# HGRN head 0: forget and query units multiplied together, cleared buffers moved, next head's units spread by halves

## The reference, cut to what matters

```python
h = h + 0.5 * swiglu(rmsnorm_2(h, ffn1_norm), ffn1_w_in, ffn1_w_out)
u = rmsnorm_2(h, mix_norm)
hq, hf, hi, hg = columns of (u @ w_in)       # 8 heads of 128 columns each
log_f = logaddexp(log(lb), log1p(-lb) + log_sigmoid(hf))
k_h = -expm1(log_f)                           # 1 - f
q_h = silu(hq) * 128 ** -0.5
# S_t = diag(f_t) S_{t-1} + k_t^T v_t ; o_t = S_t^T q_t, in chunks of 64
o_h = rmsnorm_2(o, hgrn_out_norm) * silu(hg)
```

## Time and profile before

| | us |
|---|---|
| median of 3 runs | 3306.32 (3302.76 to 3309.76) |
| the profiled execution | 3309.65 |
| its span in the trace | 3307.7 |
| start of the first matmul of head 0's F | 1693.85 |
| start of head 0's level 0 on PE | 1719.94 |
| start of head 1's level 0 on PE | 1751.44 |
| granted TensorE clock over the span | 0.984 |

### The profile page before, as it was taken

One profiled execution on the slowest core, in us unless ns is written; L12 is line 12 of the kernel. 1 busy time (PEld: TensorE's weight loads), 2 busy tenths in 40 slices (PEclk: granted clock), 3 DMA queues, 4 the chain that ended last, 5 costly groups with the idle time before them and its releaser, 6 DMA issues.

```text
span 3307.7 us, 44803 instructions
## 1 busy us (share of the span) xinstructions
PE 3184.6 (96%) x16754; PEld 2628.3 (79%) x16754; DVE 1573.9 (48%) x2197; ACT 1408.4 (43%) x2471; POOL 1587.1 (48%) x1361
## 2 busy tenths in 40 slices
PE   7889999999999999999989998999999999999998
PEld 5657888877688888788878887888888888888887
DVE  5883433136634321434148887655555543234421
ACT  3354343325843333343236565545555432243332
POOL 5345444655554457444553324444444445464454
PEclk8999999999999999999999999999999999999999
DMA  4112333341023333333332221111111123333332
GB/s 136 51 33 64 98 99 91 101 129 52 1 80 98 95 95 96 92 99 92 95 81 59 64 64 33 39 39 39 36 37 39 33 72 100 96 96 95 95 94 78
DMA packets 471621, 246.86 MB, mean 75 GB/s; under 512 B 13883, under 2 KB 468774, under 8 KB 471334
## 3 DMA queue, kind: packets, MB, share of 16 engines
q1 hardware_dynamic: 470144, 241.33, 25.6%
q10 hardware_dynamic: 1318, 3.35, 0.3%
HBM read 241.51 MB, written 2.10 MB: 74 GB/s over the span
## 4 chain that ended last, share of the span: by engine, by line
PE 85%; DVE 7%; ACT 3%; issue 3%; POOL 1%; DMA 0%; POOLq 0%; DVEq 0%; ACTq 0%
PE ps L465 19%; PE ps L466 19%; PE ps L467 19%; PE ps L2526 2%; PE ps L2415 2%; PE ps L2417 2%; PE ps L2416 2%; PE ps L2508 2%; PE ps L1655 2%; PE ps L1679 2%; PE ps L1665 2%; PE ps L1880 1%; PE ps L1882 1%; PE ps L1881 1%; PE ps L1953 1%
## 5 line engine op out<-in xcount | busy, mean ns | idle before, releaser
L447 POOL TENSOR_TENSOR w_lo<-ring,w_hi 128x512 fp32r<-128x512 f32 (+1 forms) x908 | 1224.7, 1370 | 1470.0 <-ACT w_hi L438 1469.9
L438 ACT ACTIVATE w_hi<-ring 128x512 fp32r<-128x512 f32 (+1 forms) x908 | 516.3, 617 | 1257.3 <-PE ps L467 1189.6
L465 PE MATMUL ps<-h_hi,w_hi 128*128 128x512 f32 x1776 | 700.7, 395 | 1.8 <-POOL w_lo L447 1.8
L467 PE MATMUL ps<-h_hi,w_lo 128*128 128x512 f32 x1776 | 691.4, 389 | 0.0
L466 PE MATMUL ps<-h_lo,w_hi 128*128 128x512 f32 x1640 | 638.4, 389 | 0.0
L465 PEld LDWEIGHTS ps<-h_hi,w_hi 128*128 128x128 f32 x1776 | 333.5, 188 | 76.9 <-issue 5.8
L467 PEld LDWEIGHTS ps<-h_hi,w_lo 128*128 128x128 f32 x1776 | 333.4, 188 | 69.8
L466 PEld LDWEIGHTS ps<-h_lo,w_hi 128*128 128x128 f32 x1640 | 307.9, 188 | 67.8 <-issue 4.8
L466 PE MATMUL ps<-a_lo,w_hi 128*128 128x512 f32 x752 | 292.6, 389 | 0.0
L465 PE MATMUL ps<-a_hi,w_hi 128*128 128x512 f32 x720 | 280.8, 390 | 0.0
L467 PE MATMUL ps<-a_hi,w_lo 128*128 128x512 f32 x720 | 280.2, 389 | 0.0
(11 more groups left out here) (463 smaller groups left out, 5613.8 us busy)
## 6 DMA issues: line engine op xcount, KB each, us to landing
ring<-in_ffn_w_in SPq DMA_DIRECT2D x176, 512.0 KB, 3.7
ring<-in_w_in SPq DMA_DIRECT2D x96, 512.0 KB, 3.9
ring<-in_ffn_w_down SPq DMA_DIRECT2D x32, 512.0 KB, 4.0
ring<-in_ffn_w_out SPq DMA_DIRECT2D x32, 512.0 KB, 3.8
ring<-in_w_o SPq DMA_DIRECT2D x16, 512.0 KB, 4.0
ring<-in_w_branch_gdn SPq DMA_DIRECT2D x16, 512.0 KB, 3.8
ring<-in_nsa_w_in SPq DMA_DIRECT2D x15, 512.0 KB, 3.7
ring<-in_dsa_w_in SPq DMA_DIRECT2D x13, 512.0 KB, 4.0
```

The source lines that it names most:

```text
L438: act.activation(w_hi[:, (halves(u) + j) % PIECES, 0:n, :], slot(u)[:, j * n:(j + 1) * n, :], ACT.Copy) \
L447: pool.tensor_tensor(w_lo[:, q % PIECES, 0:n, :], slot(u)[:, j * n:(j + 1) * n, :], w_hi[:, q % PIECES, 0:n, :].bitcast(f32), ALU.subtract ...
L465: pe.matmul(dst, wh, hi(k), start=first and k == 0, stop=False)
L467: ins = pe.matmul(dst, wl, hi(k), start=False, stop=last and k == 2 * n - 1)
```

## The change

Four things are changed, all of them around head 0:

1. F and Q of head 0 are multiplied together: for each tile k three matmuls of F and three of Q, into their two banks (`pe_hgrn_first_pair`). Each still signals `unit_done` with its own last matmul.
2. `lb_diff` and the memsets of `ql` and `kl` go ahead of the normalisation on DVE; `h_att` is cleared behind the forget operations of head 0, `rows` behind the last gather of head 0.
3. ACT's two sigmoids of `lb_diff` go between the root and the rounding of the tiles; the two DMA issues stay behind the rounding, without the wait for `lb_diff`.
4. In head 0, PE makes the units of head 1 as one half behind each level: F, F, Q, Q, V, V behind levels 0 to 5, and both halves of G behind level 6. ACT's and POOL's orders of units are as before, and heads 1 to 7 keep their order.

```diff
+    def pe_hgrn_first_pair(pe, ready):
+
+        n = KT // 2
+        for k in range(KT):
+            for j in (HG_F, HG_Q):
+                q = halves(hg_unit(0, j)) + k // n
+                if k % n == 0:
+                    pe.wait_ge(half_split, q + 1)
+                if j == HG_F:
+                    pe.wait_ge(*ready(k))
+                bank = ps[:, HG_BANK[j], :]
+                wh, wl = w_hi[:, q % PIECES, k % n, :], w_lo[:, q % PIECES, k % n, :]
+                pe.matmul(bank, wh, h_hi[:, k, :], start=k == 0, stop=False)
+                pe.matmul(bank, wh, m_lo_tile(k), start=False, stop=False)
+                ins = pe.matmul(bank, wl, h_hi[:, k, :], start=False, stop=k == KT - 1)
+                if k == KT - 1:
+                    ins.then_inc(unit_done.sem, 1)
...
     def pe_hgrn(pe, norm):
-        for half in range(2):
-            pe_hgrn_half(pe, 0, HG_F, half, lambda k: tile_ready(norm, k))
-        for j in (HG_Q, HG_V, HG_G):
+        pe_hgrn_first_pair(pe, lambda k: tile_ready(norm, k))
+        for j in (HG_V, HG_G):
             for half in range(2):
                 pe_hgrn_half(pe, 0, j, half)
...
-                if more and l < 2:
+                if h == 0 and l < NL:
+                    pe_hgrn_half(pe, h + 1, (HG_F, HG_Q, HG_V)[l // 2], l % 2)
+                elif h == 0:
+                    for half in range(2):
+                        pe_hgrn_half(pe, h + 1, HG_G, half)
+                elif more and l < 2:
                     pe_hgrn_half(pe, h + 1, HG_F, l)
...
-    def act_hgrn(act):
+    def act_hgrn_bounds(act):
         act.wait_ge(sig("lb_diff").sem, 1)
-        act_load_gdn(act)
         act.activation(lb, lb_diff, ACT.Sigmoid).then_inc(sig("lb_ready").sem, 1)
         act.activation(one_lb, lb_diff, ACT.Sigmoid, scale=-1.0).then_inc(sig("lb_ready").sem, 1)
+
+    def act_hgrn(act):
+        act_load_gdn(act)
...
-    def dve_hgrn(dve, ch):
+    def dve_hgrn_clear(dve):
         g0 = GAIN_ROWS["hgrn_lb_logits_2"]
         dve.wait_ge(x_ready.sem, after_ffn1)
...
-        dve.memset(rows[0:64, :], 0.0).then_inc(sig("rows_clear").sem, 1)
         dve.memset(ql, 0.0)
         dve.memset(kl, 0.0)
-        ch.link(dve.memset(h_att, 0.0))
+
+    def dve_hgrn(dve, ch):
         dve.wait_ge(sig("lb_ready").sem, 2)
...
         dve_hgrn_forget(dve, ch, 0)
+        ch.link(dve.memset(h_att, 0.0))
         dve_hgrn_query(dve, 0)
...
             gather(h, NL)
+            if h == 0:
+                dve.memset(rows[0:64, :], 0.0).then_inc(sig("rows_clear").sem, 1)
             if h + 1 < HG_HEADS:
                 dve_hgrn_forget(dve, ch, h + 1)
...
-            act_norm(act, plans["mix_norm"])
+            act_root(act, plans["mix_norm"])
+            act_hgrn_bounds(act)
+            act_split(act, plans["mix_norm"])
             act_hgrn(act)
...
+            dve_hgrn_clear(dve)
             dve_norm(dve, ch, plans["mix_norm"], lo=m_lo_tile)
             dve_hgrn(dve, ch)
```

## The result

| | before | changed |
|---|---|---|
| median of 20 runs | 3307.05 (3299.73 to 3310.77) | 3313.03 (3304.00 to 3316.07) |
| profiled execution | 3309.65 | 3313.51 |
| its span | 3307.7 | 3311.3 |

The ratio is 1.0017, 95% interval 1.0010 to 1.0024: the change costs about 5.6 us, just under the 0.2% that I called the bound of what can be told, and the twenty runs of each side do tell it from nothing. Forecast were +3.4 us and 3309.7.

A forecast was written before the change was run, and what follows sets the result against it. PE, busy 96% of the span, was taken to bound the kernel. Terms 0.6 + 1.3 + 1.5 = +3.4 us on a median of 3306.3 gave 3309.7, range 3301.3 to 3314.5.

The forecast's parts named there:

- The clearing: Ahead of DVE's normalisation: `lb_diff` waits for POOL, so reciprocal, tiles and PE's start come 0.75 us late; bounds 0 and 1.9.
- F and Q together: Head 0's start on PE: no late tiles, the pair takes 13.5 us, a gain of 1.65 us before the later start.
- The wait for V: After head 0's F and Q, PE waits 1.62 us for V's halves, giving back the gain of 1.65 us.
- DVE's level 0 was ready about 1.2 ahead of PE and stays so: Head 0's level 0: DVE keeps its margin of about 1.2 us, so level 0 comes only 0.6 us later.
- Units one half per level: Head 0's levels: waits of 0.45 ahead of level 3 and 3.6 ahead of G replace 2.64; +1.3 us.
- The clock: Behind the wait ahead of head 1's G: some 3.0 us of matmuls at half speed, +1.5 us; bounds 0 and 3.4.
- The clock did not stay up: Rival: the clock stays up at the wait ahead of head 1's G; +1.9 us, 3308.2; chance 0.17.
- the gain did not stay: Rival: a new wait, ahead of V or G, is absent; +1.8, -1.6 or about -3.8 us; chance 0.12.
- the clock falls more than once: Rival: low clock also behind V's wait (1.7 us) and longer at G (1.9 us); +7.0, 3313.3; chance 0.11.
- Even so it can't reach -6.6: all that could be had is 4.33 + 2.64 = 7.0: Limit on savings at head 0's F and ahead of level 5: the change cannot become 6.6 us faster.
- What head 0 gains or loses is carried to the end: Heads 1 to 7 have next to no slack on PE, so head 0's shift reaches the total unchanged.

The follow-up runs named there:

- V's early half: Changed kernel, but ACT rounds head 0's V's first half as soon as F's first half has been multiplied: 3311.23 us, one execution.
- F, F, Q, Q: Kernel before with only F and Q of head 1 as halves behind levels 0 to 3, V and G behind level 6: 3301.17 us, ratio 0.9979.
- the old order: Changed kernel with head 1's units in the order of the kernel before (V and G behind level 6): 3311.80 us, ratio 1.0013.

## Why the prediction was right

The forecast, a small loss within 0.2%, held: 3313.0 against a range of 3301.3 to 3314.5. The waits and the low clock it was made of are there. That the total came within some 2 us of the sum is in part luck: the stretch behind head 1, which the forecast took as fixed, differed by 6.8 us between profiles of this one kernel. By its own steps:

- *The clearing.* Forecast 0.75 late, measured 0.55. `lb_diff` waited for POOL's first operation (1.12 in place of 0.15), the memsets didn't (0.91 each). The Trainium skill, "SBUF — State Buffer", section "Who interferes with whom", says that a DVE instruction with two SBUF inputs contends with a GpSimd instruction that reads SBUF, and one with at most one, outside the two-port modes, does not; the trace agrees, with these numbers.
- *F and Q together.* Forecast 13.5 us, or 13.35 with the later start (0.6 at the end for 0.75 at the beginning); measured 13.24 (1691.83 to 1705.07, the last matmul's start at 1704.84 and 0.227). No tile was late.
- *The wait for V.* Forecast 1.62, measured 1.60 by the same count (1705.07 to 1706.67; the 1.45 of the profile begins where the last matmul's record ends). It brought no low clock: from 1706.70 to 1718.00 the granted clock is 1.00. V's early half shows the cause.
- *"DVE's level 0 was ready about 1.2 ahead of PE and stays so"* failed. PE waited 0.48 for it, and level 0 came 1.0 late in place of 0.6. Costs were missing: POOL's two splits now run in one row and the forget step's three operations take 4.2 us in place of 2.2, DVE's first two differences take 2.8 in place of 0.8, and the memset of `h_att` (0.91 + 0.16) lies in DVE's chain. The memset's move stands in the list of changes; the prediction costed neither it nor POOL's row against that margin.
- *Units one half per level.* Forecast +1.3 with waits of 0.45 and 3.6; measured 0.24 and 3.06. Without the low clock the head took 8.37 - 5.5 = 2.9 less than its 35.4, so 32.5 against 31.5, +1.0. The wait of 3.06 is 0.54 under the forecast in three small parts: level 6's product took 1.05 and not 0.9, its gather came 1.09 behind it and not 1.20, and from the gather to the gate it took 2.29 and not 2.57, mostly because the memset of `rows` held DVE for 0.41 and not 0.64. The waits alone explain 0.7 of the +1.0 (0.24 + 3.06 for 2.64); the other 0.3 lies in the matmuls of the finer order.
- *The clock.* The term that was mis-sized: forecast 1.5, measured 2.9 in each of three profiles, within its bounds of 0 to 3.4. I took a low stretch of 3.0 us; it was 6.3 us of G's products. With V's half early the same wait of 3.06 cost 1.7, near the forecast.
- *The rivals.* The clock did not stay up, and the gain did not stay. Of *the clock falls more than once* one half came, the long low stretch at G (1.4 more than my sum has, for the 1.9 of the rival); the other, a low clock behind V's wait, did not.
- *"Even so it can't reach -6.6: all that could be had is 4.33 + 2.64 = 7.0"* does not follow, since 7.0 is more than 6.6, and it failed in fact: F, F, Q, Q, which only fills the 2.64, is 6.9 us under the kernel before.

The sum up to head 1 is thus +4.8 in place of +3.4. The total's 5.6 (3.3 to 7.9) holds that.

*"What head 0 gains or loses is carried to the end"* was the weakest step, and the result alone would not have shown it. PE has indeed next to no slack in heads 1 to 7, but behind them the waits of the second branch are followed by a low clock more or less often. How much of the changed kernel's loss came from there is open: low clock rose from about 104 to 108 us over the runs, no more than the low stretch behind its own gate's wait can explain, but behind head 1's level 0 its three profiles took 1.4 more, 5.3 less and 1.5 more than the one of before, so either sign was possible. Where its two times some 5 us apart come from is thus seen; why the same head 0 is followed by the one or the other wasn't settled.

## What to carry to other kernels

A unit of work that covers a wait is spent when it is moved: V was moved, with Q's second half, to fill 2.64 us ahead of level 5, which Q's half fills alone, and its going uncovered 3.06 ahead of G. Move only as much as the gap needs, and ask what the moved piece stood in front of. Work whose buffers are freed together (two units multiplied tile by tile) takes away the cover for the next unit's preparation; free them by halves. Where a program has many waits of 2 to 3 us on TensorE, a change of a microsecond can't be judged by the total time alone: look at the stretch itself, and shift it by a known amount of idle work to see how much of the total is the clock behind other waits.

## What the runs showed of the hardware

- Equal waits of TensorE are followed by a low clock or not: 2.22 us by 0.58 or 1.00, 2.64 us by 1.00 before and by 0.60 with the old order. 3.06 us was followed by a low clock in four profiles of four, 0.53 over 6.3 us in three of them and over 3.5 us in one.
- Adding 1.3 us of matmuls made one version 5.3 us faster (4.6 by the ratios), adding 2.1 us made another 9.2 slower (8.9).
- A VectorE operation on 8 columns with two inputs in SBUF took 1.12 us beside a GpSimd subtraction and 0.15 alone; `tensor_scalar` on 512 columns took 1.39 and 1.51 beside GpSimd and 0.43 and 0.48 alone; a memset took 0.91 either way.
